# Sample caches and retention state laid out by position, moved in one transfer each, keys loaded as the stage begins

## What is computed

```
kk = concatenate([cache_swa_k, ks], axis=1)          # 8 x 129 x 2 x 64
swa_k_s = kk[:, -WINDOW:]                            # 8 x 128 x 2 x 64
new_state = state * exp(L * lg) + einsum('blhd,blhe->bhde', k * k_decay, v)
```

## Time and profile before

| | |
|---|---|
| median of 3 runs | 3156.43 us (3151.49 to 3164.68) |
| the profiled execution, its own time | 3157.23 us |
| its span, first to last instruction | 3155.4 us |
| busy: PE / DVE / POOL / ACT | 2280.7 / 2025.5 / 1184.3 / 1029.9 us |
| DMA: bytes, mean rate over the span | 1217.33 MB, 386 GB/s |
| of it the gathers (software queue) | 1082.20 MB |
| of it SP's transfers (hardware queue) | 133.27 MB |
| mean granted clock of TensorE | 0.845 of full speed |

### The profile page before, as it was taken

The page is one execution under the profiler, slowest core; times in us unless marked ns, Lnnn a source line. Parts: engine busy times, 40 slices in busy tenths (PEclk is TensorE's granted clock), DMA queues, the critical chain, the costliest instruction groups (busy, mean ns, idle before and its releaser), DMA issues.

```text
span 3155.4 us, 29062 instructions
## 1 busy us (share of the span) xinstructions
PE 2280.7 (72%) x8766; PEld 977.8 (31%) x8766; DVE 2025.5 (64%) x4948; ACT 1029.9 (33%) x3292; POOL 1184.3 (38%) x1052
## 2 busy tenths in 40 slices
PE   7889769886798874756686577756785688568565
PEld 5667424552245421232221132212221222111111
DVE  3273546875478544768558865797568756866864
ACT  3312422334223432313432343225323343233221
POOL 0011334434343341424344444444444444444442
PEclk9999989998899977867798788868887889789867
DMA  8478999999999996979999999999999999999996
GB/s 307 152 256 292 423 421 406 417 419 411 422 406 420 384 418 269 375 281 409 424 421 402 415 421 421 407 403 420 421 405 406 415 412 413 411 397 421 421 411 276
DMA packets 202766, 1217.33 MB, mean 386 GB/s; under 512 B 25656, under 2 KB 52560, under 8 KB 68336
## 3 DMA queue, kind: packets, MB, share of 16 engines
q0 software_dynamic: 148608, 1082.20, 83.4%
q1 hardware_dynamic: 54000, 133.27, 11.5%
HBM read 1189.26 MB, written 21.54 MB: 384 GB/s over the span
## 4 chain that ended last, share of the span: by engine, by line
DMA 40%; PE 30%; DVE 11%; issue 5%; SPq 5%; ACT 4%; POOL 3%; POOLq 0%; DVEq 0%; ACTq 0%
DMA ring<-in_peer_uv,idxg 36%; PE ps L884 13%; PE ps L861 7%; DVE ring L1578 6%; PE ps L646 5%; POOL ring L572 3%; SPq L405 3%; ACT ring L955 2%; DMA wo<-in_w_in 1%; SPq L399 1%; PE ps L842 1%; PE ps L621 1%; DMA out<-work 1%; PE ps L662 1%; DVE proj L1500 1%
## 5 line engine op out<-in xcount | busy, mean ns | idle before, releaser
L572 POOL DMA_INDIRECT ring<-in_peer_uv,idxg x1024 | 1170.2, 1143 | 1712.4 <-PE ps L884 1470.9
L884 PE MATMUL ps<-ring 128*64 128x512 f32 x4096 | 1248.3, 742 | 666.7 <-ACT ring L955 665.3
L1578 DVE SCALAR_TENSOR_TENSOR ring<-ring,xlo 128x1024 f32<-128x1024 f32 x512 | 627.1, 1225 | 539.7 <-DMA ring<-in_peer_uv,idxg 534.8
L1578 DVE SCALAR_TENSOR_TENSOR ring<-ring,xhi 128x1024 f32<-128x1024 f32 x512 | 626.8, 1224 | 396.5 <-DMA ring<-in_peer_uv,idxg 389.9
L884 PEld LDWEIGHTS ps<-ring 128*64 128x64 f32 x4096 | 292.0, 159 | 1475.9 <-ACT ring L955 998.5
L1125 ACT ACTIVATE small<-small 128x2 f32<-128x2 f32 x512 | 104.0, 203 | 1703.9 <-DVE ring L1578 1703.5
L646 PE MATMUL ps<-wo 128*128 128x176 f32 x1792 | 306.0, 329 | 62.4 <-ACT wo L955 27.9
L646 PEld LDWEIGHTS ps<-wo 128*128 128x128 f32 x1792 | 283.7, 199 | 119.2 <-issue 96.7
L955 ACT ACTIVATE ring<-gdiag,small 128x64 f32<-128x64 f32 x1024 | 300.3, 340 | 16.8
L955 ACT ACTIVATE gdiag<-fold,gateg 128x64 f32<-128x64 f32 x1024 | 292.8, 333 | 1.5
L861 PE MATMUL ps<-keyw,work 128*128 128x512 f32 (+1 forms) x576 | 266.6, 607 | 1.1 <-ACT work L955 1.1
(11 more groups left out here) (198 smaller groups left out, 1526.9 us busy)
## 6 DMA issues: line engine op xcount, KB each, us to landing
wo<-in_w_in SPq DMA_DIRECT2D x48, 704.0 KB, 8.3
ring<-in_peer_uv,idxg POOLq DMA_INDIRECT x1024, 12.3
wo<-in_w_out SPq DMA_DIRECT2D x4, 4096.0 KB, 17.6
ring<-in_w_in SPq DMA_DIRECT2D x8, 1408.0 KB, 7.9
proj_scratch<-wo SPq DMA_DIRECT2D x112, 88.0 KB, 9.5
proj<-proj_scratch SPq DMA_DIRECT2D x7, 1408.0 KB, 12.2
ring<-in_wqT SPq DMA_DIRECT2D x16, 512.0 KB, 3.6
h<-in_x_prompt SPq DMA_DIRECT2D x10, 512.0 KB
```

Of the source, the lines that this page charges most:

```text
L572: nc.gpsimd.indirect_dma_start(row[r], None, A["peer_uv"], bass.IndirectOffsetOnAxis(ap=experts, axis=0)).then_inc(ld_row[r], 16)
L884: mm = nc.tensor.matmul(acc[side * HP:(side + 1) * HP, n * 512:(n + 1) * 512], row_u[r][:, 0:HP], row_v[r][:, n * 512:(n + 1) * 512], star ...
L1578: ins = stt(row_u[r], row_u[r], 1.0, (xlo, xhi)[unit % 2][:], ALU.mult, ALU.mult, accum_out=dot[:, r:r + 1])
```

## The change

The host hands over the caches as 128 positions x (8 samples x 128 numbers), shifted by one position, so that positions 1 to 127 lie in rows 0 to 126 and the last row is free for the new one (it holds the dropped position until then). The state is handed over as 128 x (8 x 4 x 128). The outputs 5, 6 and 7 have the same layouts and are put back in order by the host. Each of the six transfers (both caches in and out, state in and out) becomes one DMA with the shape of its SBUF tile.

The load of the keys moves from behind the merging of the quarters to the beginning of the stage, behind the loads of the quarters and the rotation table. The quarters move to columns 5376 to 8192, off the place of `kw`. The load of the values comes right behind the store of the new keys and values, before the wait for it. SP waits for each cache load before it loads the new row over the last partition. The new row of the values has a tick of its own, SAMPLE_AT + 14.

```
--- before.py
+++ after.py
@@ -223,7 +223,7 @@
 
         part = space(wof)
         projs, ropes = part(D_IN), part(256)
-        quarters = wof[:, D_IN + 256:2 * D_IN + 256]
+        quarters = wof[:, KC * D - D_IN:]
         sT, ss, sr, pts, osT = part(96), part(64), part(P), part(64), part(32)
         prod = part(512)[0:NS, :]
         kw, vw, kwT = part(D).rearrange("p (s c) -> p s c", s=NS), part(D).rearrange("p (s c) -> p s c", s=NS), part(D)
@@ -392,18 +392,17 @@
                 late_stored(len(PIECES))
                 sp.dma_start(quarters, quarters_d).then_inc(sm["quarters"], 16)
                 sp.dma_start(ropes[0:NS, :], A["c_rope"][SEQ:NTOK, :]).then_inc(sm["columns"], 16)
+                sp.dma_start(kw, A["cache_swa_k"]).then_inc(sm["kw"], 16)
                 yield SAMPLE_AT + 9
                 sp.wait_ge(sm["merged"], 3)
                 sp.dma_start(proj_d[SEQ:NTOK, C_KS:D_IN], projs[0:NS, C_KS:D_IN]).then_inc(sm["own_kv"], 16)
-                for s in range(NS):
-                    sp.dma_start(kw[0:P - 1, s, :], A["cache_swa_k"][s, 1:P].rearrange("w k d -> w (k d)")
-                                 ).then_inc(sm["kw"], 16)
+                sp.dma_start(vw, A["cache_swa_v"]).then_inc(sm["vw"], 16)
                 sp.wait_ge(sm["own_kv"], 16)
+                sp.wait_ge(sm["kw"], 16)
                 sp.dma_start(kw[P - 1:P, :, :], proj_d[SEQ:NTOK, C_KS:C_VS].rearrange("(a s) c -> a s c", a=1)
                              ).then_inc(sm["kw"], 16)
-                for s in range(NS):
-                    sp.dma_start(vw[0:P - 1, s, :], A["cache_swa_v"][s, 1:P].rearrange("w k d -> w (k d)")
-                                 ).then_inc(sm["vw"], 16)
+                yield SAMPLE_AT + 14
+                sp.wait_ge(sm["vw"], 16)
                 sp.dma_start(vw[P - 1:P, :, :], proj_d[SEQ:NTOK, C_VS:D_IN].rearrange("(a s) c -> a s c", a=1)
                              ).then_inc(sm["vw"], 16)
                 sp.dma_start(out[3][0].rearrange("w k d -> w (k d)"), proj_d[SEQ - P:SEQ, C_KS:C_VS]
@@ -411,20 +410,18 @@
                 sp.dma_start(out[4][0].rearrange("w k d -> w (k d)"), proj_d[SEQ - P:SEQ, C_VS:D_IN]
                              ).then_inc(st_misc, 16)
                 yield SAMPLE_AT + 20
-                sp.wait_ge(sm["kw"], 16 * (NS + 1))
-                sp.dma_start(out[6].rearrange("s w k d -> w s (k d)"), kw).then_inc(st_misc, 16)
-                sp.wait_ge(sm["vw"], 16 * (NS + 1))
-                sp.dma_start(out[7].rearrange("s w k d -> w s (k d)"), vw).then_inc(st_misc, 16)
+                sp.wait_ge(sm["kw"], 32)
+                sp.dma_start(out[6], kw).then_inc(st_misc, 16)
+                sp.wait_ge(sm["vw"], 32)
+                sp.dma_start(out[7], vw).then_inc(st_misc, 16)
                 yield SAMPLE_AT + 47
                 sp.wait_ge(sm["ov"], 1)
                 sp.wait_ge(st_misc, 64)
-                sp.dma_start(st_s.rearrange("p s h e -> p (s h) e"),
-                             A["state_ret"].rearrange("s h d e -> d (s h) e")).then_inc(sm["st_in"], 16)
+                sp.dma_start(st_s, A["state_ret"]).then_inc(sm["st_in"], 16)
                 sp.dma_start(sel8[0:NS, :], A["c_sel8"]).then_inc(sm["st_in"], 16)
                 yield SAMPLE_AT + 91
                 sp.wait_ge(sm["st"], 1)
-                sp.dma_start(out[5].rearrange("s h d e -> d (s h) e"), st_s.rearrange("p s h e -> p (s h) e")
-                             ).then_inc(st_state, 16)
+                sp.dma_start(out[5], st_s).then_inc(st_state, 16)
 
             def move_tokens(b):
 
@@ -685,7 +682,7 @@
                 for j in range(4):
                     t = T(SA[:, 64 + j * NS:64 + (j + 1) * NS], projs[0:NS, C_QS + j * P:C_QS + (j + 1) * P], NS)
                 t.then_inc(sm["qT"], 1)
-                pe.wait_ge(sm["kw"], 16 * (NS + 1))
+                pe.wait_ge(sm["kw"], 32)
                 for s in range(4):
                     t = T(SB[:, s * P:(s + 1) * P], kw[:, s, :])
                 t.then_inc(sm["kwT"], 1)
@@ -712,7 +709,7 @@
                 T(SA[:, 288:352], sr[0:64, :], 64).then_inc(sm["pT"], 1)
                 yield SAMPLE_AT + 46
                 pe.wait_ge(sm["pT_out"], 1)
-                pe.wait_ge(sm["vw"], 16 * (NS + 1))
+                pe.wait_ge(sm["vw"], 32)
                 ov = SA[:, 352:384].rearrange("p (c s) -> p c s", c=4)
                 pv = pts.rearrange("p (s j a b) -> p s j a b", s=NS, j=KVH, a=2)
                 for s in range(NS):
@@ -1665,8 +1662,8 @@
 
 _INS = ["x_prompt", "x_sample", "state_ret", "cache_swa_k", "cache_swa_v", "norm1_g", "swa_sinks", "w_out",
         "norm2_g", "final_g"]
-_OUTS = [(1, SEQ, D), (NS, 1, D), (1, RH, HD, HD), (1, P, KVH, SD), (1, P, KVH, SD), (NS, RH, HD, HD),
-         (NS, P, KVH, SD), (NS, P, KVH, SD)]
+_OUTS = [(1, SEQ, D), (NS, 1, D), (1, RH, HD, HD), (1, P, KVH, SD), (1, P, KVH, SD), (HD, NS, RH, HD),
+         (P, NS, KVH * SD), (P, NS, KVH * SD)]
 
 
 def constants():
@@ -1718,10 +1715,17 @@
     arrays["sub_keysT"] = np.ascontiguousarray(
         np.asarray(inputs["peer_sub_keys"]).transpose(3, 0, 1, 2).reshape(NK, NSC))
     arrays["peer_uv"] = np.concatenate([np.asarray(inputs["peer_u"]), np.asarray(inputs["peer_v"])], axis=1)
+    for name in ("cache_swa_k", "cache_swa_v"):
+        later = np.roll(np.asarray(inputs[name]), -1, axis=1)
+        arrays[name] = np.ascontiguousarray(later.transpose(1, 0, 2, 3).reshape(P, NS, KVH * SD))
+    arrays["state_ret"] = np.ascontiguousarray(np.asarray(inputs["state_ret"]).transpose(2, 0, 1, 3))
     arrays.update(constants())
     args = {n: nc.dram_tensor("in_" + n, a.shape, mybir.dt.from_np(a.dtype), kind="ExternalInput").ap()
             for n, a in arrays.items()}
     outs = [nc.dram_tensor(f"out_{i}", shape, F32, kind="ExternalOutput").ap() for i, shape in enumerate(_OUTS)]
     build(nc, args, outs)
     r = _run(nc, [{"in_" + n: a for n, a in arrays.items()}], core_ids=[0])
-    return tuple(r.results[0][f"out_{i}"] for i in range(len(_OUTS)))
+    got = [r.results[0][f"out_{i}"] for i in range(len(_OUTS))]
+    got[5] = got[5].transpose(1, 2, 0, 3)
+    got[6], got[7] = (kept.transpose(1, 0, 2).reshape(NS, P, KVH, SD) for kept in got[6:8])
+    return tuple(got)
```

## The result

The changed kernel took a median of **3103.7 us** (3101.6 to 3110.6, 4 runs) against 3154.5 for the kernel before (3151.5 to 3164.7, 4 runs). The ratio is 0.985, with a 95% interval of 0.983 to 0.987: 51 us less. Predicted were 3104, between 3091 and 3122. The 3104 were reckoned from the profiled execution before (3157.2 us); the profiled executions differ by 53.6 us, the medians by 51. The profiled execution took 3103.6 us, its span is 3101.8.

The account below looks back on a forecast made before the run. DMA's gathers of expert rows were taken to set the pace, with block 2 losing 62.6 us to stalls. Savings of 29.7 + 1.5 + 17.8 + 3.6 = 52.6 us off 3157.2 gave 3104 us, range 3091 to 3122.

Parts of the forecast that it names:

- the three waits: PE's waits in block 2: 29.7 us before the key transposes, 22.2 before the value matmuls, 7.1 before the state matvecs.
- the ceiling of 62.6 us: Block 2's DMA time lost against 421 GB/s, summed over its stages: the most this change could win back.
- One engine for 127 rows, one turn for each row: Old cache loads: 127 rows use one DMA engine of 16, each row getting one turn, 0.313 us, after each gather row.
- The rival of an unseen layout: Cache and state transfers: packets stay at 512 bytes, 20 us per cache, new key row late; 3120 us, chance 0.04.
- The new key row: Before the key transposes: the row's store and load end at 1226, just before PE; saves 29.7 us, bounds 18 to 30.2.
- The rival of a late row: At the key transposes: PE waits 12 us for the new row instead of 0.5; 3116 us, chance 0.08.
- Score stretch: Block 2 from 1266 to 1302, where PE limits: 1.5 us saved of 6.0 lost, bounds 0 to 6.
- Value and state load: Waits at the value matmuls and before the state matvecs: 17.8 us saved of 18.8 lost, bounds 13 to 18.8.
- Matvecs: DMA loss behind PE's state matvecs: 7.6 us before, 4 left, so 3.6 saved.
- DVE as the next bound: Second half of block 2: DVE, put at 87% busy, fits; as a rival it binds, 3112 us, chance 0.05.
- A fixed price per transfer: Rival: gain is only 14 transfers saved at 2.95 us each, 3116 us (3129 by the skill's formula); chance 0.03.
- Large packets: Rival: packets of 4 and 16 KB hold up the gathers for 42 us; 3199 us, chance 0.02.

Follow-up runs that it names:

- the 127-row kernel: The changed kernel with each cache load bringing 127 rows of 4 KB instead of 128, still in one transfer: 3155.1 us, ratio 1.001.
- the eight transfers of 128: The changed kernel with each cache loaded in eight transfers, one per sample, of 128 rows of 512 bytes: 3115.0 us, ratio 0.988.
- the second profile: The changed kernel itself run once more, unaltered, beside the kernel with split matvecs and later DVE steps: 3103.9 us, ratio 0.985.
- the keys loaded late: The changed kernel with its one key transfer issued behind the store of the new keys and values: 3103.4 us, ratio 0.985.
- the attempts to win the last 7 us: The changed kernel with state matvecs split into four groups: 3103.9 us; then also with dependent DVE steps 3 slots later: 3102.9 us, rerun 3098.3.
- the state alone: The kernel before with only the state's load and store changed to 128 rows of 16 KB: 3147.6 us, ratio 0.999.
- the early load: The kernel before with only its eight key loads of 127 rows moved to the beginning of the stage: 3154.0 us, ratio 1.001.
- the caches without the state: The changed kernel with the state's load and store put back in the old layout of 512-byte runs: 3119.3 us, ratio 0.990.

## Why the prediction was right, point by point

The mechanism held: the three waits went, and DMA runs at full rate where it stood. That the time is met to the microsecond is luck: one term was 2.9 us too large and three others together 2.9 too small.

- **What bounds the kernel, and the ceiling of 62.6 us:** held. The blocks behind kept their lengths, and the losses of DMA before and after account for the whole difference.
- **One engine for 127 rows, one turn for each row:** shown by the 127-row kernel (60 us for the keys worked out, at most 68 measured) and by the eight transfers of 128 (20 us for the values, 22.7). It was read from two numbers of the trace, 0.07 of DMA and 39.8 us for 127 rows.
- **Packets of full rows:** held, by the balance of 8416 packets. The rival of an unseen layout falls.
- **The new key row:** the step gave 7 us for the store and 10.1 for the row, PE just met. Measured were at most 4.4, and at most 6.5: both were oversized, the row had over 5 us in hand, and the loss is zero in place of 0.5. The rival of a late row falls here, though the eight transfers show how near it is: 10.5 us of wait cost 11, so almost nothing hides such a wait.
- **Score stretch:** 1.5 saved by forecast; 2.7 are left of 6.0, so 3.3. What is left is a dip of its own (325 GB/s from 1260 to 1272); the prediction's signs named only the one behind the matvecs.
- **Value and state load:** 17.8 by forecast, 18.4 measured. The cover of four pairs took 22.5 us (from 1313.2 to 1335.7), 20 were worked out. What I had not seen is that this part leans on the layout of the state, with 13 us of block 2 or 16 of the time; my working put the state's load at some 8 us in the rival of an unseen layout.
- **State's store:** 12.8 us, 12 worked out, and as forecast it was worth nothing: block 3 took 346.9 us, before 347.3.
- **Matvecs:** 3.6 saved by forecast, 0.7 measured (6.9 left of 7.6, 6.8 in the second profile). The clock did come up a little (10.7 us in place of 13.8), but the gathers in flight last no longer than before. With the keys loaded late the matvecs took 13.8 us again at 0.50, and block 2 was no longer for it. This term was the worst sized; its 2.9 us too much cancel against what the new row, the scores and the values gave beyond their terms.
- **DVE as the next bound:** the forecast had 87% for the end of block 2; it is 106.2 of 125, 85%. But right behind the matvecs it is close to full, and the attempts to win the last 7 us ended there.
- **A fixed price per transfer**, with its 3116 to 3129: as the source of the gain it is ruled out by one row of 128, and by the eight transfers, which cost 11 us and not 41. The formula that the prediction takes from the Trainium skill (DMA: Bandwidth & Descriptors, Anatomy of one DMA) is given there for transfers issued from GpSimd; these are SP's, so the 3129 was an estimate from another path.
- **Large packets:** with 128 rows over 16 engines DMA kept its full rate (421 GB/s from 1182 to 1213, around the key load); with 127 on one it fell to 328.

Whether the parts add up is open. By the times they don't: the state alone brings 4 us and the early load 0, the caches without the state 33 (3119.3 against 3151.8), and all together 51. By the length of block 2 they do: the state alone 15.0, the caches without it 41.1, all 54.3.

## What to carry to other kernels

Look at the count of partitions in a transfer before its bytes: 127 went down one engine of 16, and beside a full queue of large gathers each of its rows waited for one of theirs. A row that is overwritten anyhow is worth loading. Look on SP's timeline for issues of tens of microseconds: here they belonged to transfers whose rows waited on one engine, and the profile blamed the small transfer behind them. And price each part of a change in the kernel that the other parts leave behind, with enough runs for its size: to take the state's layout back out of the changed kernel cost 16 us, while the gain of the same layout on the kernel before could not be told from nothing.

## What the runs showed of the hardware that I had not expected

- A load of 4096 runs of 512 bytes (the state, before) went as 1024 packets of 2 KB, its store of the same runs as 4096 packets of 512 bytes: 1204 packets with 2.17 MB passed the hardware queue from 1370 to 1386 with that load in it, 4112 with 2.10 MB from 1480 to 1542 with the store alone.
- Large rows on one engine slow the whole of the traffic: 328 GB/s from 1216 to 1242 with 127 rows of 4 KB on one engine, 421 from 1182 to 1213 with 128 rows on all.
- Small transfers landed sooner under full gathering than I had thought: at most 4.4 us for 8 KB to DRAM, at most 6.5 for one row of 4 KB.
